# A two-layer encoder with a 32-expert feed-forward on one core: token-major router logits, alternating halves in the slots product, and six rotating weight places

## What is computed

```python
h = rms_norm(x, ln2_g[l]) * (1.0 + sc2) + sh2
x = x + g2 * hier_moe(h, ...)

def hier_moe(h, rg_w, rg_b, re_w, re_b, w_gate, w_up, w_down):
    pg = softmax(ht @ rg_w + rg_b)                    # 4 groups
    pg_top, g_sel = top_k(pg, 1)
    le = (ht @ re_w + re_b).reshape(T, 4, 8)          # 32 experts
    top_v, top_i = top_k(le of the chosen group, 2)
    gate = pg_top * softmax(top_v)
    # every token goes to its 2 experts:
    # y += gate * ((silu(x @ w_gate[e]) * (x @ w_up[e])) @ w_down[e])
```

## Time and profile before

| | us |
|---|---|
| median of 3 runs | 1601.35 (1600.17 to 1603.58) |
| the profiled execution | 1594.81 |
| its span in the trace | 1593.0 |

### The profile page before, as it was taken

How to read it: one execution, slowest core, us unless ns; L and a number is a source line. 1 busy time by engine, 2 the same in 40 slices (tenths; PEclk the granted TensorE clock), 3 DMA queues, 4 the chain that set the end, 5 groups by cost and what they waited for, 6 DMA issues and landing times.

```text
span 1593.0 us, 18145 instructions
## 1 busy us (share of the span) xinstructions
PE 1338.2 (84%) x6748; PEld 759.2 (48%) x6748; DVE 617.1 (39%) x1442; ACT 364.6 (23%) x825; POOL 268.8 (17%) x248
## 2 busy tenths in 40 slices
PE   5899999987895798889969999998779769987862
PEld 1446556645542454444434665664454345544441
DVE  4734433477624222432262343246762432211111
ACT  1311024454401111112111202254440211110101
POOL 0201200000000343323210120000000125332321
PEclk8999999999997899999968999999999879999995
DMA  8810222645457599999651122143116668999954
GB/s 299 290 35 19 96 79 80 237 160 154 168 185 316 205 330 378 411 402 408 219 218 40 53 96 79 62 177 132 54 48 226 264 233 313 402 403 406 398 198 183
DMA packets 98609, 336.76 MB, mean 211 GB/s; under 512 B 28370, under 2 KB 33106, under 8 KB 73272
## 3 DMA queue, kind: packets, MB, share of 16 engines
q1 hardware_dynamic: 74712, 305.52, 49.3%
q0 software_dynamic: 15072, 16.85, 4.7%
q10 hardware_dynamic: 8736, 13.21, 2.4%
HBM read 324.08 MB, written 28.98 MB: 222 GB/s over the span
## 4 chain that ended last, share of the span: by engine, by line
PE 70%; DVE 12%; ACT 7%; issue 5%; DMA 4%; POOL 1%; SPq 1%; ACTq 0%; DVEq 0%; POOLq 0%
PE bank L495 65%; DMA big<-in_moe_w_down_dram 2%; PE bank L773 2%; ACT pr_r L1404 2%; PE bank L870 2%; DVE pr_r L2067 2%; ACT pr_r L1451 1%; DVE pr_r L1935 1%; DVE pr_r L2070 1%; DMA big<-in_ada_w_dram 1%; PE bank L610 1%; DVE pr_r L1720 1%; DVE big L1676 1%; DVE small L1919 1%; DVE pr_r L1918 1%
## 5 line engine op out<-in xcount | busy, mean ns | idle before, releaser
L495 PE MATMUL bank<-big,pr_r 128*64 128x256 f32 (+2 forms) x3192 | 453.1, 403 | 88.4 <-issue 26.4
L495 PEld LDWEIGHTS bank<-big,pr_r 128*64 128x64 f32 (+1 forms) x3192 | 273.5, 152 | 239.9 <-issue 113.4
L495 PE MATMUL bank<-big,ht_r 128*128 128x512 f32 (+3 forms) x832 | 308.0, 555 | 1.9 <-ACT ht_r L1417 1.9
L495 PEld LDWEIGHTS bank<-big,ht_r 128*128 128x128 f32 (+1 forms) x832 | 143.8, 189 | 137.3 <-issue 126.0
L495 PE MATMUL bank<-big 128*128 128x256 f32 (+4 forms) x496 | 168.9, 478 | 18.5 <-DVE big L1860 5.7
L1591 POOL DMA_INDIRECT x_rows<-ht_r,slot_i x64 | 102.0, 1593 | 326.0 <-DVE ht_r L2073 312.4
L2067 DVE TENSOR_TENSOR pr_r<-pr_r,bank 64x256 f32<-64x256 f32 x65 | 27.5, 423 | 256.2 <-ACT pr_r L1451 238.4
L495 PEld LDWEIGHTS bank<-big 128*128 128x128 f32 (+2 forms) x496 | 91.6, 197 | 61.5 <-issue 29.7
L1451 ACT ACTIVATE pr_r<-bank 64x256 f32<-64x256 f32 x64 | 24.1, 377 | 410.8 <-PE bank L495 410.8
L1527 POOL TENSOR_SCALAR small<-small 128x1 f32<-128x1 f32 (+2 forms) x20 | 10.1, 504 | 598.2 <-DVE small L1899 336.5
L2073 DVE SCALAR_TENSOR_TENSOR ht_r<-bank,mix_r,mod 128x512 f32<-128x512 f32 x65 | 48.8, 751 | 132.6 <-PE bank L495 132.6
(11 more groups left out here) (298 smaller groups left out, 1215.0 us busy)
## 6 DMA issues: line engine op xcount, KB each, us to landing
big<-in_moe_w_gate_dram SPq DMA_DIRECT2D x63, 1024.0 KB, 14.7
big<-in_moe_w_up_dram SPq DMA_DIRECT2D x63, 1024.0 KB, 20.9
big<-in_moe_w_down_dram SPq DMA_DIRECT2D x63, 1024.0 KB, 25.5
big<-in_ada_w_dram SPq DMA_DIRECT2D x16, 3072.0 KB, 11.5
big<-in_w_in_dram SPq DMA_DIRECT2D x4, 3072.0 KB, 11.1
big<-in_w_out_dram SPq DMA_DIRECT2D x4, 2048.0 KB, 8.7
mod<-in_ada_b_dram SPq DMA_DIRECT2D x12, 512.0 KB, 10.1
big<-in_w_in_dram SPq DMA_DIRECT2D x2, 2048.0 KB, 8.1
```

The source lines that it names most:

```text
L495: return nc.tensor.matmul(o, l, r, start=start, stop=stop)
```

## The change

- **Logits.** PE now has a tile's `hT` slice (128 tokens) as the stationary operand and streams the 36 columns of `r_w`. The result has tokens on the partitions, so `lgT`, ACT's bias step and the four transposes are gone. Each tile's logits stand between the row transposes of later tiles. The bias `r_b` is now loaded as a broadcast row (ACT's queue) and added by DVE in the copy. SP's `load_router` is gone.
- **Slots product.** The two halves of rows alternate, piece by piece. It has only the first two tables (64 columns); the weights table has a product of its own behind it ("wslots", 32 columns), after `wtab_ready`. DVE sets `hot_ready` before it writes `w_of`, and sums `cnt` after it.
- **Places.** In layer 1 all six places rotate. In layer 0 the order of the places stays. The over block's weights go to place 0 instead of 3.

```diff
-        EXPERT_SLOT = [2, 3, 0, 1, 4, 5] + [(2, 3, 0, 1)[i % 4] for i in range(NE - 6)]
+        SIX = (2, 3, 0, 1, 4, 5)
+        EXPERT_SLOTS = [list(SIX) + [SIX[i % 4] for i in range(NE - 6)], [SIX[i % 6] for i in range(NE)]]
...
-        OVER_SLOT = [3] * DEPTH
+        OVER_SLOT = [0, 0]
...
+                lg_bank = V.bank("lg")
+                def logits(t):
+                    taken(pe, f"hT{NT + t}1")
+                    for k in range(KT):
+                        last = mm(lg_bank[:, t * 36:(t + 1) * 36], hT[:, k, t * P:(t + 1) * P], r_w[:, k, :], k == 0, k == KT - 1)
+                    return last
+                pe.wait_ge(rw_in, 96 * l + 16 * 6)
+                logits(0)
                 transpose_rows(2 * NT - 2)
+                logits(1)
                 transpose_rows(2 * NT - 1)
-                taken(pe, f"hT{2 * NT - 1}1")
-                pe.wait_ge(rw_in, 64 * l + 16 * 4)
-                b = A.bank("lgT")
-                for k in range(KT):
-                    last = mm(b[0:36, :], r_w[:, k, :], hT[:, k, :], k == 0, k == KT - 1)
-                last.then_inc(ready_a, 1)
-                taken(pe, "lgT")
-                b = V.bank("lg")
-                for t in range(NT):
-                    last = nc.tensor.transpose(b[:, t * 36:(t + 1) * 36], lgT[:, t * P:(t + 1) * P], ident[0:36, 0:36])
-                last.then_inc(ready_v, 1)
+                logits(2)
+                logits(3).then_inc(ready_v, 1)
...
-                for rows in (slice(0, CAP), slice(CAP, P)):
-                    for k in range(2):
-                        for t in range(NT):
-                            last = mm(b[rows, 0:3 * NE], rank_is[:, k, t], row_tab[:, k, t].rearrange("p j e -> p (j e)"),
+                for k in range(2):
+                    for t in range(NT):
+                        for rows in (slice(0, CAP), slice(CAP, P)):
+                            last = mm(b[rows, 0:2 * NE], rank_is[:, k, t], row_tab[:, k, t, 0:2].rearrange("p j e -> p (j e)"),
                                       k + t == 0, k + t == NT)
+                last.then_inc(ready_v, 1)
+                pe.wait_ge(wtab_ready, l + 1)
+                b = V.bank("wslots")
+                for k in range(2):
+                    for t in range(NT):
+                        for rows in (slice(0, CAP), slice(CAP, P)):
+                            last = mm(b[rows, 0:NE], rank_is[:, k, t], w_of[:, k, t], k + t == 0, k + t == NT)
                 last.then_inc(ready_v, 1)
...
-                took(nc.vector.tensor_copy(slot_w, b[:, 2 * NE:3 * NE]))
+                b = V.take("wslots")
+                took(nc.vector.tensor_copy(slot_w, b[:, 0:NE]))
```

More of the change, by code:

```diff
@@ L202, in rb @@
             return at(mix_r, o, *dims, rows=rows)
-        lgT = rb(S, rows=36)
+        parts_room = rb(S)
         lg = rb(NT, 36)
@@ L431, in trunk @@
                 chunk_at[l, c] = (i, loaded[i])
-            for e, i in enumerate(EXPERT_SLOT):
+            for e, i in enumerate(EXPERT_SLOTS[l]):
                 loaded[i] += 48
@@ L436, in before_in_slot @@
         def before_in_slot(e):
-            return max((n for n in range(e) if EXPERT_SLOT[n] == EXPERT_SLOT[e]), default=None)
+            slots = EXPERT_SLOTS[in_layer[0]]
+            return max((n for n in range(e) if slots[n] == slots[e]), default=None)
         def last_in_slot(s):
-            return max(n for n in range(NE) if EXPERT_SLOT[n] == s)
+            return max(n for n in range(NE) if EXPERT_SLOTS[in_layer[0]][n] == s)
         def chunk_slot(c):
@@ L1432, in layer @@
                 evac(2 * NT - 1)
-                b = R.take("lgT")
-                A_(lgT, b[0:36, :], ACT.Identity, bias=r_b).then_inc(taken_a, 1)
                 act.wait_ge(e_in, 2 * l + 1)
@@ L2021, in layer @@
                 step(nc.vector.tensor_copy(cum, low))
-                step(RED(cnt, b[:, P:2 * P].rearrange("p (t e) -> p e t", t=NT), X, ALU.add))
                 for k in (3, 2, 1):
-                    last = TT(cum[:, NT - k:NT], cum[:, NT - k:NT], tot[:, 0:k], ALU.add)
-                    if k > 1:
-                        step(last)
-                took(last)
+                    step(TT(cum[:, NT - k:NT], cum[:, NT - k:NT], tot[:, 0:k], ALU.add))
                 for k, mk in ((0, m1), (1, m2)):
@@ L2032, in layer @@
                     TT(rank_is[:, k], iota_c.unsqueeze(1).to_broadcast([P, NT, CAP]), up(rank_f[:, k], CAP), ALU.is_equal)
-                    TT(id_of[:, k], mk, up(tok_id, NE), ALU.mult)
+                    last = TT(id_of[:, k], mk, up(tok_id, NE), ALU.mult)
+                last.then_inc(hot_ready, 1)
+                for k, mk in ((0, m1), (1, m2)):
                     last = TT(w_of[:, k], mk, up(wgt[:, k], NE), ALU.mult)
-                last.then_inc(hot_ready, 1)
+                last.then_inc(wtab_ready, 1)
+                took(RED(cnt, b[:, P:2 * P].rearrange("p (t e) -> p e t", t=NT), X, ALU.add))
                 step(STT(out=cum, in0=cum, scalar=float(NE), in1=iota_e.unsqueeze(1).to_broadcast([P, NT, NE]), op0=ALU.mult, op1=ALU.add))
```

37 lines of the change are left out of this document (17 added, 20 removed).

## The result

The changed kernel takes 1554.88 us in the median of 4 runs (1552.68 to 1555.77), the kernel before 1600.76 (1595.6 to 1603.58, 4 runs): ratio 0.9715, interval 0.9688 to 0.9742, so 45.9 us less. The forecast was 1557, in a range from 1547 to 1573. The profiled executions have spans of 1593.0 and 1550.8 us, 42.2 apart.

What follows compares the result with a forecast made beforehand. It took TensorE to bound nearly everywhere, and the DMA from expert 16 of layer 1 on. Router 14.2, change of layers 9.3, rotation 7.4 and over block 13.4 sum to 44.3 us: 1601.35 - 44.3 = 1557, range 1547 to 1573.

Steps and rivals of the forecast that it cites:

- Logits: Router: the new logits product lets DVE's add start 7.5 us earlier in layer 1 and 8.3 in layer 0.
- the clock stays: Router logits: TensorE priced at 2.4 GHz, a tile costing 2.1 us; at 1.2 GHz up to 4.0.
- rival (a): Router logits: clock stays at 1.2 GHz, a tile costs 4.0 us, total gain 33, 1568 us; chance 0.20.
- Tables and slots product: Router: tables save 0.7 us a layer; slots product takes 3.4 us, gaining 1.4 in layer 1 and 0.9 in layer 0.
- The new wait on the weights: Router: DVE's `slot_w` copy waits for the new 2.6 us weights product, delaying expert 0; cost 1.4 us, range 0.3 to 2.8.
- The late gather: Router: expert 0's gather, issued at about 1277.3 among weight loads, lands at 1283.5 and sets expert 0's transposes at 1283.6.
- Change of layers: Between layers: waves load earlier, so PE's 9.36 us wait ahead of 32 instructions goes; gain 9.3 us, bounds 7 and 12.
- Rotation: Layer 1 experts: expert 10 waits for expert 4, not 6; the train comes 7.4 us earlier, bounds 3 and 8.
- Over block: End of kernel: its weights land right behind expert 31's and its product runs at full clock; gain 13.4 us.
- (b): Layer 1 experts: the DMA pause gives nothing back because gathers and table writes fill it; 1564 us, chance 0.12.
- (c): Change of layers: something else holds PE at once (scatter landing, mod sums); 1566 us, chance 0.09.
- Rival (d): Layer 1 experts: with six places gathers queue behind more loads, a step takes 13 us, not 8.7; 1638 us, chance 0.02.

Runs made afterwards that it cites:

- logits_only: Kernel before with only the new logits (tokens as stationary operand, bias added by DVE): 1594.0 us, ratio 0.9957.
- halves_alternate: Kernel before with the slots product's 32 instructions alternating between column halves, still 96 columns, weights not split off: 1584.42 us, one run.
- after_again: The changed kernel, unchanged, run again on chip 12: 1556.94 us, ratio 0.9732 to the kernel before.
- fill_and_hold: Changed kernel plus trimmed unneeded PE products in the router, and expert 5's weights held until expert 0's gather landed: 1548.71 us, ratio 0.9687 to before.
- keep_clock: Changed kernel plus unneeded identity products in all of PE's router waits, to hold the clock: 1551.71 us, ratio 0.9757 to the kernel before.
- keep_clock_logits: Changed kernel plus unneeded identity products only behind logits 0 and logits 1: 1552.40 us, ratio 0.9759 to the kernel before.
- over_only: Kernel before with only the over block moved to place 0 in both layers: 1576.99 us, ratio 0.9853.
- rotate_only: Kernel before with only all six places taking turns in layer 1, over block still in place 3: 1590.52 us, ratio 0.9939.

## Why the prediction was right, and where it was right by luck

The sum was 44.3 us, measured were 45.9 and, on chip 12, 41.8. That it comes so close is luck. By the stages of chip 1 (the gather by the changed kernel) the logits gave 10.4 us less than their term and the over block 1.2 less, and the slots product, the gather, the change of layers and the rotation gave 3.4, 2.4, 2.9 and 2.7 more: 11.6 against 11.4. The mechanisms of points 5 to 7 below were right, the one of point 1 was not. Point 1 rests on this row of the kernel before too, which stands between the first two of the earlier trace rows:

```profile
1252.35 1.98 PE L610 MATMUL bank<-ident,big 128*128 128x128 f32 x8 [3.08 <-DVE big L1726]
```

By its steps:

1. **Logits: 15.8 forecast, 5.4 in the routers of logits_only (1.9 and 3.5).** The step that failed is "the clock stays": rival (a) describes the layer, with a tile of 3.3 to 3.5 us instead of its 4.0. I had given it 0.20, although the kernel before has the slow time for eight transposes (1.98 us instead of 1.12) at 1255.40 and already at 1252.35, behind a gap of 3.08 us at the same place. The new order shortens the gap to 1.37 us and fills the rest with short products, and that was not enough; with 256-column products in the gaps, which close them too, it was. A granted clock of 0.50 through the logits was the first of the forecast's own signs of being wrong. Layer 0's term also took the old product's 10.01 us as its price, and the same product took 8.4 to 9.4 us there in the other five profiles that have it. TensorE: Matmul & The Clock Gate (the Trainium skill, Part 4) says that transposes don't count as activity for the clock. By that rule rival (a) was the likelier case; the traces agree with its result, though no run here tells the transposes from the 36-column products between them, nor either from the gap.
2. **Tables and slots product: forecast 0.7 us in layer 1 without the gather, measured 2.2; in layer 0 2.1.** Two terms were mis-sized. I took 3.4 and 2.6 us for the two products one after the other, and they take 3.63 together; I let the stationary loads of the two halves queue, and halves_alternate shows that they don't (2.83 us for what took 4.80 at the same clock). I also read the 4.15 us of the earlier trace rows as a price at low clock; the granted clock was 0.60 on average there. TensorEngine Tiling (the Trainium skill, section Theoretical Speedup) gives up to two times here; the trace agrees at 1.7. The new wait on the weights was real but small: DVE waited 0.71 us for the second product.
3. **The late gather: 1.2 us forecast a layer, 0 measured**, for the logits left it time; once they didn't, expert 0 waited 3.8 to 5.0 us for it, of which 0.4 would have gone to DVE's list anyway. The mechanism was right and its size too small.
4. Together the two routers gave 9.9 us (from the unchanged ones of chip 1 to after_again) to 11.9 (between the two profiles) against 14.2: an error of 10.4 us in the logits, and of 3.4 and 2.4 the other way in the slots and the gather.
5. **Change of layers: 9.3 forecast (7 to 12); 12.2 on chip 1**, of which 10.6 at the filters, and 8.7 on chip 7 (281.0 to 272.3, with other edits in it). The waves were there first, as argued, so PE did not even stop at the filters, and at full clock the 32 filter products take 15.67 us instead of 16.65.
6. **Rotation: 7.4 forecast (3 to 8); 10.1 on chip 1**, 5.4 on chip 7 (251.2 to 245.8, again with other edits). The term is between the two. The difference is the stall. From SP's issue of expert 6's weights to expert 31's product it is 242.7 to 243.5 us with four places and no stall, and 246.8 to 248.3 with it. With six places it is 236.8 and 237.6 without the stall and 237.1 to 237.9 with it (fill_and_hold, which holds 3 MB back, has 239.0). So there the stall costs nothing, for the DMA's share is 1.02 or 1.03 in every stretch of 20 us from 1290 to 1490 us of the changed kernel: the DMA alone sets the pace there. The rotation gives 5.1 to 6.7 us without the stall and about 10 with it. What issues expert 6's load earlier does arrive: in keep_clock it goes out 5.1 us behind expert 0's transposes instead of 8.2 in keep_clock_logits, and that is 3.1 of the 3.9 us between their "experts 1". One reading in this step was off too: the 9.5 us of spacing run from a landing to a product's start, and between products give 8.7, by which the term would be 8.1.
7. **Over block: 13.4 forecast, 12.2 to 12.8 measured.** Right in place, mechanism and size.

Smaller slips of the working change nothing: the low bound of the new wait in step 2 comes out at 0.5 instead of 0.3, the gather's new issue at 1277.1 instead of 1277.3, and PE's waits for weights from expert 16 on are 0.7 to 2.4 us instead of 1 to 2.

So rivals (b) and (c) are out: over_only and rotate_only show that nothing held PE at the change of layers and that removing the pause gives back 5 us or more. Rival (d) as well: the rotation alone is 10 us faster. The first two profiles compare a kernel without the stall with one that has it; alone they give 8.1 us for experts and change in layer 0 and 5.9 for the rotation, where chip 1, with the stall on both sides, gives 12.2 and 10.1.

What stays open: what the stall at expert 3 is. It starts 29 to 31 us behind expert 0's transposes in both layers, whatever stood ahead in the program, on two of three chips. No run was made on its cause. Open too is which of gap, transposes and short products costs the clock.

## What to carry over

Cut two traces at the same marks and compare stretches, and repeat the profile of the kernel before on the same chip before you call a difference of a few us a cost of the edit. A step that is taken off the critical path arrives only as far as the next latest thing lets it: here the gather came next, and the routers gave the clock's gain back only when 3 MB of weights were moved out of its way. In this kernel short products between gaps did not keep TensorE's clock. Ask in which of its two levels a moved product will run before its price is taken from a row.

## What the runs showed of the hardware

- Products on alternating column halves run side by side including their stationary loads: 32 of 96 columns in 2.83 us instead of 4.80 at 1.2 GHz; 32 of 64 columns and 32 of 32 columns together in 3.63 at 1.2 GHz and 2.06 at 2.4 GHz, and the narrower half of them takes as long as the wider (1.9 and 2.0).
- A gap of 1.37 us among transposes and 36-column products was followed by a fall of the granted clock to 0.50, which then held for 37 us, through the rest of the router and its longer gaps (6.27, 3.71 and 3.51 us); with four 256-column products (1.97 us) in place of the first gap the clock stayed at 1.00 through the logits.
- A product whose stationary operand is 128 columns and whose moving one 36 costs 0.12 us at 2.4 GHz and 0.21 at 1.2.
- The same kernel before has medians of 1591.6, 1598.7 and 1600.5 us on three chips, and a stall of 2.4 to 2.6 us at one place of each layer shows in every profile of two of them and in none of the third (each chip was used once).
